# State products that leave one operand in a bank, two projection steps ahead of them, and GpSimd's low parts behind the written state

## The reference

```python
def _s5_direction(u_ctx, u_lat, lam, dt, bmat, cmat):
    lam_dt = lam * dt[:, None]
    lam_bar = jnp.exp(lam_dt)
    b_bar = ((lam_bar - 1.0) / lam)[..., None] * bmat
...
    def step(h, u_chunk):
        bu = jnp.einsum('btgs,gps->btgp', u_chunk.astype(jnp.complex64), b_bar)
        a = jnp.broadcast_to(lam_bar, bu.shape)
        _, xs = lax.associative_scan(_ssm_combine, (a, bu), axis=1)
        xs = xs + powers[None] * h[:, None]
        y = jnp.einsum('btgp,gsp->btgs', xs, cmat).real
        return xs[:, -1], y
```

## Time and profile before

| | |
|---|---|
| median of 3 runs | 2220.47 us (2219.76 to 2221.86) |
| the profiled execution | 2218.46 us, span 2216.7 us |
| TensorE busy | 2086.7 us (94%) |
| VectorE busy | 1271.0 us (57%) |
| ScalarE busy | 766.5 us (35%) |
| POOL busy | 632.0 us (29%) |
| granted TensorE clock | 0.981 of full |
| the S5 states | first product at 1358.5 us, last written at 1662.6 us |

### The profile page before, as it was taken

How to read it: one execution, slowest core, us unless ns; L and a number is a source line. 1 busy time by engine, 2 the same in 40 slices (tenths; PEclk the granted TensorE clock), 3 DMA queues, 4 the chain that set the end, 5 groups by cost and what they waited for, 6 DMA issues and landing times.

```text
span 2216.7 us, 38909 instructions
## 1 busy us (share of the span) xinstructions
PE 2086.7 (94%) x15596; PEld 1510.8 (68%) x15596; DVE 1271.0 (57%) x1896; ACT 766.5 (35%) x1425; POOL 632.0 (29%) x1129
## 2 busy tenths in 40 slices
PE   7999898999998999999989978999979999999997
PEld 6887777755554555555556547888867788888785
DVE  3366664459994444444467766999992333333334
ACT  3335543231103444444410036544444332222223
POOL 2643111500016888888701211111121000000000
PEclk9999999999999999999999989999999999999999
DMA  9221443423452111111135425999964233323321
GB/s 359 83 88 60 145 154 124 161 79 121 164 180 86 53 53 53 53 55 70 53 143 212 164 79 151 299 301 297 291 206 150 86 96 97 102 96 95 96 86 38
DMA packets 119411, 292.42 MB, mean 132 GB/s; under 512 B 11616, under 2 KB 57056, under 8 KB 113088
## 3 DMA queue, kind: packets, MB, share of 16 engines
q1 hardware_dynamic: 107072, 226.10, 31.4%
q0 software_dynamic: 12160, 63.84, 7.8%
HBM read 223.97 MB, written 65.93 MB: 131 GB/s over the span
## 4 chain that ended last, share of the span: by engine, by line
PE 82%; DVE 10%; issue 3%; ACT 3%; POOL 1%; DMA 0%; SPq 0%; DVEq 0%; ACTq 0%; POOLq 0%
PE psum L470 29%; PE psum L1867 8%; PE psum L2563 7%; PE psum L2306 5%; PE psum L2342 5%; PE psum L2737 4%; PE psum L2317 3%; PE psum L1142 3%; PE psum L2331 2%; PE psum L2387 2%; PE psum L2378 2%; DVE early L2937 2%; PE psum L304 2%; DVE early L2917 2%; DVE const L2950 1%
## 5 line engine op out<-in xcount | busy, mean ns | idle before, releaser
L470 PE MATMUL psum<-split,w_split 128*128 128x512 f32 x1632 | 371.5, 389 | 0.0
L470 PEld LDWEIGHTS psum<-split,w_split 128*128 128x128 f32 x1632 | 306.3, 188 | 63.7
L452 DVE TENSOR_TENSOR w_split<-ring,w_split 128x512 fp32r<-128x512 f32 x182 | 129.0, 709 | 309.3 <-ACT w_split L447 308.9
L2088 POOL TENSOR_TENSOR early<-early 128x8 f32<-128x8 f32 (+6 forms) x672 | 277.6, 413 | 52.8
L447 ACT ACTIVATE w_split<-ring 128x512 fp32r<-128x512 f32 x182 | 115.1, 633 | 337.0 <-PE psum L470 334.0
L1867 PE MATMUL psum<-early,ring 128*128 128x512 f32 (+1 forms) x544 | 176.5, 486 | 0.0
L2563 PE MATMUL psum<-gate,ring 128*128 128x512 f32 (+1 forms) x512 | 165.4, 486 | 1.2 <-issue 1.2
L2737 PE MATMUL psum<-h,u_w 128*128 128x256 f32 (+1 forms) x768 | 151.7, 349 | 15.1 <-ACT u_t L2651 11.4
L1867 PEld LDWEIGHTS psum<-early,ring 128*128 128x128 f32 x544 | 103.7, 191 | 71.8 <-issue 64.7
L2563 PEld LDWEIGHTS psum<-gate,ring 128*128 128x128 f32 x512 | 97.2, 190 | 69.3 <-issue 62.7
L470 PE MATMUL psum<-h,w_split 128*128 128x512 f32 x552 | 134.5, 404 | 8.0 <-DVE w_split L452 8.0
(11 more groups left out here) (439 smaller groups left out, 3511.9 us busy)
## 6 DMA issues: line engine op xcount, KB each, us to landing
ring<-in_s_glu SPq DMA_DIRECT2D x64, 512.0 KB, 3.5
ring<-in_w_mod SPq DMA_DIRECT2D x48, 512.0 KB, 5.8
made_c_pow<-area POOLq DMA_DIRECT2D x16, 1152.0 KB, 5.0
c_pow<-made_c_pow SPq DMA_DIRECT2D x32, 576.0 KB, 5.3
ring<-in_s_in SPq DMA_DIRECT2D x32, 512.0 KB, 6.4
made_b_pow<-area POOLq DMA_DIRECT2D x15, 1024.0 KB, 4.5
b_pow<-made_b_pow SPq DMA_DIRECT2D x15, 1024.0 KB, 10.2
ring<-in_w_in SPq DMA_DIRECT2D x25, 512.0 KB, 3.6
```

The source lines that it names most:

```text
L452: nc.vector.tensor_tensor(rounded(buffer(u, 1)), source(u), buffer(u, 0), ALU.subtract).then_inc(dve_done, 1)
L470: ins = nc.tensor.matmul(out, rounded(buffer(u, w)[:, ks]), values(x, k), start=(first and k == 0 and n == 0), stop=(last and k == UNIT_K ...
L2088: nc.gpsimd.tensor_tensor(o, a, b, op).then_inc(pool_done, 1)
```

## The change

Seven things change, all in the S5 stage.

1. The sine product comes first, and the cosine product is written back over its input in the banks. The add and the subtract read the one operand from the banks and the other from `mod_s`. `x_read` is counted at the subtract, not at the second product.
2. The decay has two buffers, ScalarE makes it first in its turn for a quad, and waits for the scan two quads back.
3. `x_pe(q + 1)` stands behind two projection steps; each half of a tile has four steps.
4. POOL waits for the written state of quad u - 8 before it makes the low part of unit u.
5. `y_out` has one half as its only buffer; its room goes to the second decay. The GELU of tile m waits for the store of tile m - 1.
6. The other small tiles in the same room move.
7. A second memset clears the first column of the second decay.

```diff
@@ -2612,17 +2612,17 @@
         s5 = ExitStack()
         eye = const[:, len(MASKS) * P + N_LAGS + 8 * C_LAT:len(MASKS) * P + N_LAGS + 8 * C_LAT + GS]
         lag_m = early_part(0, 2048).rearrange("p (b g c) -> p b g c", b=2, c=P)
-        y_out = early_part(2048, 1024).rearrange("p (b t) -> p b t", b=2)
-        y_tm = early_part(3072, 1024).rearrange("p (s c) -> p s c", s=STEP)
-        b_pow_t = early_part(4096, 1024).rearrange("p (b j c) -> p b j c", b=2, c=P)
-        s5_tmp = early_part(5120, 16 * C_ALL)
+        y_out = early_part(2048, 512)
+        y_tm = early_part(2688, 1024).rearrange("p (s c) -> p s c", s=STEP)
+        b_pow_t = early_part(3712, 1024).rearrange("p (b j c) -> p b j c", b=2, c=P)
+        s5_tmp = early_part(4736, 16 * C_ALL)
         b_bar_split = early_part(B_SPLIT, 4 * TPD * GS).rearrange("p (r t e i) -> p r t e i", r=2, t=TPD, e=2)
         c_pow = sb(s5, "c_pow", [2, 2, TPD, STEP + 1, GS])
         b_pow = sb(s5, "b_pow", [2, 2, TPD, STEP, GS])
         table = sb(s5, "table", [2, 2, TPD, C_ALL])
         u_w = sb(s5, "u_w", [4, 2, HALF_SLOT])
         u_t = sb(s5, "u_t", [2, TPD, C_CTX + C_ALL])
-        decay = sb(s5, "decay", [4, C_ALL])
+        decay = [sb(s5, "decay", [4, C_ALL]), early_part(6272, 4 * C_ALL).rearrange("p (g c) -> p g c", g=4)]
         u_cm = [sb(s5, "u_cm", [STEP, C_CTX + C_ALL]), early_part(6656, 1024).rearrange("p (s c) -> p s c", s=STEP)]
@@ -2681,7 +2681,9 @@
                     rest(k - 1)
             rest(KD - 1)
 
-            v.memset(decay[:, :, 0:1], 0.0).then_inc(dve_done, 1)
+            v.memset(decay[0][:, :, 0:1], 0.0).then_inc(dve_done, 1)
+            dve_count.up()
+            v.memset(decay[1][:, :, 0:1], 0.0).then_inc(dve_done, 1)
             dve.wait_ge(dve_done, dve_count.up("s5", "decay_zero"))
 
         def eye_dve(dve):
@@ -2873,10 +2875,10 @@
         def decay_act(act, q):
             if q >= QUADS:
                 return
-            if q >= 1:
-                act.wait_ge(*at("s5", "scanned", q - 1))
+            if q >= 2:
+                act.wait_ge(*at("s5", "scanned", q - 2))
             for g in range(4):
-                nc.scalar.activation(decay[:, g, 1:C_ALL], mask("ones")[:, 1:C_ALL], ACT.Copy,
+                nc.scalar.activation(decay[q % 2][:, g, 1:C_ALL], mask("ones")[:, 1:C_ALL], ACT.Copy,
                                      scale=decay8[:, 4 * q + g:4 * q + g + 1]).then_inc(act_done, 1)
                 act_count.up("s5", "decay", q)
 
@@ -2922,19 +2924,19 @@
                                           .broadcast_to([P, 2, 4, b - a]))
             dve.wait_ge(*ready(table_ready[h], m))
             dve.wait_ge(*at("s5", "x", q))
-            v.tensor_tensor(mod_c, x, both_parts(0, 0, C_ALL), ALU.mult).then_inc(dve_done, 1)
+            v.tensor_tensor(mod_s, x, both_parts(1, 0, C_ALL), ALU.mult).then_inc(dve_done, 1)
             dve_count.up()
-            tt(mod_s, x, both_parts(1, 0, C_ALL), ALU.mult, "s5", "x_read", q)
-            v.tensor_tensor(mod_c[:, 0, :, :], mod_c[:, 0, :, :], mod_s[:, 1, :, :], ALU.add).then_inc(dve_done, 1)
+            tt(x, x, both_parts(0, 0, C_ALL), ALU.mult)
+            v.tensor_tensor(mod_c[:, 0, :, :], x[:, 0, :, :], mod_s[:, 1, :, :], ALU.add).then_inc(dve_done, 1)
             dve_count.up()
-            tt(mod_c[:, 1, :, :], mod_c[:, 1, :, :], mod_s[:, 0, :, :], ALU.subtract)
+            tt(mod_c[:, 1, :, :], x[:, 1, :, :], mod_s[:, 0, :, :], ALU.subtract, "s5", "x_read", q)
             if between is not None:
                 between()
             dve.wait_ge(*at("s5", "decay", q))
             zs = mod_s
             for ri in range(2):
                 line = lambda ap: ap[:, ri, :, :].rearrange("p g c -> p (g c)")
-                v.tensor_tensor_scan(line(zs), decay[:, :, :].rearrange("p g c -> p (g c)"), line(mod_c), 0.0,
+                v.tensor_tensor_scan(line(zs), decay[q % 2][:, :, :].rearrange("p g c -> p (g c)"), line(mod_c), 0.0,
                                      ALU.mult, ALU.add).then_inc(dve_done, 1)
                 dve_count.up("s5", "scanned", q)
             dve.wait_ge(*at("s5", "scanned", q))
@@ -2996,15 +2998,16 @@
 
         def y_turn_act(act, m):
             act.wait_ge(*at("s5", "y_turned", m))
-            if m >= 2:
-                act.wait_ge(y_stored[m % 2], 16 * (m // 2))
-            nc.scalar.activation(y_out[:, m % 2, :], bank(Y_TURN_BANK),
+            if m >= 1:
+                act.wait_ge(*ready(y_stored, m - 1))
+            nc.scalar.activation(y_out, bank(Y_TURN_BANK),
                                  ACT.Gelu_apprx_tanh).then_inc(act_done, 1)
             act.wait_ge(act_done, act_count.up("s5", "yT", m))
 
 
 
-        TOKENS = (((0, 1, 2), (3, 4)), ((5,), (6, 7)))
+        STEPS_FIRST = ((0, 1), (4, 5))
+        STEPS_BEHIND = (((2,), (3,)), ((6,), (7,)))
 
         def s5_pe(pe):
             for k in range(KD):
@@ -3019,12 +3022,14 @@
                 turn_pe(pe, n)
             for q in range(QUADS):
                 m, h = divmod(q, TILE_QUADS)
+                for k in STEPS_FIRST[h]:
+                    u_project_pe(pe, m + 3, k)
                 x_pe(pe, q + 1)
                 if h == 0 and m > 0:
                     y_turn_pe(pe, m - 1)
                 for n in range(2):
                     turn_pe(pe, 2 * q + 4 + n)
-                    for k in TOKENS[h][n]:
+                    for k in STEPS_BEHIND[h][n]:
                         u_project_pe(pe, m + 3, k)
                 if h == 0:
                     lags_pe(pe, m + 1)
@@ -3054,6 +3059,7 @@
             turn_act(act, 3)
             for q in range(QUADS):
                 m, h = divmod(q, TILE_QUADS)
+                decay_act(act, q + 1)
                 if h == 0 and m > 0:
                     y_turn_act(act, m - 1)
                 turn_act(act, 2 * q + 4)
@@ -3065,7 +3071,6 @@
                     u_act(act, m + 3)
                 else:
                     lags_act(act, m + 1)
-                decay_act(act, q + 1)
                 y_act(act, q)
             y_turn_act(act, KE - 1)
             for u in range(2 * (KE + GATES_AHEAD - 1), 2 * (KE + GATES_AHEAD)):
@@ -3074,6 +3079,8 @@
         def s5_pool(pool):
             last = 2 * (KE + GATES_AHEAD - 1)
             for u in range(4, last):
+                if u >= 8:
+                    pool.wait_ge(*at("s5", "x_in", u - 8))
                 u_w_pool(pool, u)
                 if u % 2 == 1 and u >= 11:
                     y_store_pool(pool, u // 2 - 5)
@@ -3082,12 +3089,12 @@
                 u_w_pool(pool, u)
             for i in range(2):
                 pool.wait_ge(y_stored[i], 16 * KE // 2)
-            nc.gpsimd.memset(y_out[:, 0, 0:1], 0.0).then_inc(pool_done, 1)
+            nc.gpsimd.memset(y_out[:, 0:1], 0.0).then_inc(pool_done, 1)
             pool.wait_ge(pool_done, pool_count.up("s5", "y_stored"))
 
         def y_store_pool(pool, m):
             pool.wait_ge(*at("s5", "yT", m))
-            pool.dma_start(io["y"][m], y_out[:, m % 2, :]).then_inc(y_stored[m % 2], 16)
+            pool.dma_start(io["y"][m], y_out).then_inc(y_stored[m % 2], 16)
 
         FIRST_LAST = KE - 7
 
```

## The result

The changed kernel takes 2202.14 us (median of 4 runs, 2199.6 to 2205.66) against 2220.85 for the kernel before: ratio 0.9917, 95% interval 0.99 to 0.9934. The forecast was 2202. The number is right, but part of that is luck: in the stage that changes, the forecast put a gain of 18.4 us, and the profiles show 15.3. Two wrong terms cancel in part, two more are off, and the medians differ by some 3 us more than the stage does, which no part of the change explains. Which parts of the change earn the gain also came out otherwise than the text above suggests.

The account below looks back on a forecast made before the run. VectorE was taken to set S5's pace at 18.9 us a tile, TensorE close behind. Gains of 5.9 (tiles 0 to 8), 5.9 (9 to 12) and 6.6 us (13 to 15), together 18.4, took 2220.5 to 2202; range 2194 to 2213.

Parts of the forecast that it names:

- VectorE is stalled 1.0 us a quad by POOL: S5 state products: POOL's low part blocks one all-SBUF product, losing 1.0 us a quad, 2.0 us a tile.
- TensorE becomes the bound: S5 tiles: VectorE's need falls from 18.9 to 15.8 us, so TensorE's 18.05 us a tile binds.
- TensorE's work is the same: Projection steps moved to four a half: TensorE stays at 18.05 us a tile, or 17.8 if pipeline ends overlap.
- The store of y costs 0.2 us a tile: Single `y_out`: the GELU waits for the previous tile's store, making tiles 18.25 us.
- The room of 5.5 us: Single `y_out`: a store of y may take 5.5 us to land unseen; earlier stores had a median of 5.7.
- Bank writes at nothing: Cosine product written into the banks: no extra VectorE time, with 0.8 us a quad kept for the range.
- ScalarE's decay and the lags: VectorE's waits of 0.60 us for the decay and 0.54 us for the lags both go, leaving 15.8 us a tile.
- Who sets POOL's start: Where TensorE leads, ScalarE's rounding sets POOL's start, 1.5 to 3 us into the next state; up to 1.3 us blocked.
- The tail: Tiles 13 to 15, led by VectorE: six stalls of 1.0 us and some 0.6 us idle go, gaining 6.6 us.
- Tile 0: Counted among tiles 0 to 8, each going from 18.9 to 18.25 us, together 5.9 us.
- Transfers as the bound: Rival: DMA can't feed S5 tiles in under 18.9 us, giving 2210.5 us; chance 10%.
- The clock: Behind S5 TensorE runs at its lower level, granted 0.54; no gain counted, up to 3 us at the low end.

Follow-up runs that it names:

- f: The kernel before with only TensorE's new order: four projection steps a half, two ahead of `x_pe`; 2205.0 us, ratio 0.9931.
- e: The changed kernel with its products back in SBUF and `x_read` counted at the second product; 2203.1 us, ratio 0.993.
- h: The changed kernel with the old order of projection steps and the products back in SBUF; 2203.2 us, ratio 0.993.
- n: The changed kernel with three projection steps ahead of `x_pe` and one behind the first transposition; 2206.8 us, ratio 0.9947.
- c: The kernel before with one edit only, POOL's wait for the written state before each low part; 2199.0 us, ratio 0.9909.
- g: The kernel before with POOL's wait for the state and the four projection steps of a half in one run; 2203.7 us, ratio 0.9932.
- m: The changed kernel with the four projection steps of a half in one run behind `x_pe` and products back in SBUF; 2199.4 us, ratio 0.9916.
- d: The changed kernel without POOL's wait for the written state; 2201.6 us, ratio 0.9924.

## Why the prediction was right, and where it was not

*VectorE is stalled 1.0 us a quad by POOL: right.* In every kernel that moves the low part behind the written state, by the wait or by the order, the state products fall to 0.43 us at most (f keeps two long ones). Where the low part then meets an add, a scan or L2142 with its operands in SBUF, that one is held. The Trainium skill says the same ("SBUF — State Buffer", "Who interferes with whom"): two SBUF inputs contend with a GpSimd instruction that reads SBUF, one doesn't. The traces agree: e and the changed kernel are the pair that shows it, 1.18 against 0.56 us for the add.

*TensorE becomes the bound: right.* It is busy 18.40 of 18.40 us.

*"TensorE's work is the same", 18.05 us a tile: this step failed.* The same matmuls took 18.43 us. In the old order, with no wait left, they take 17.77 (h), the 17.8 that the prediction had in brackets: so the 18.05 of before held some 0.3 us of pipeline ends, as the profile models them, at its two waits. The new order costs 0.66 us a tile: two more runs of steps 0.35, y ahead of steps 0.20, L2907 behind steps 0.10. Shown by h, f (the order alone gives 18.42) and n.

*The store of y costs 0.2 us a tile: wrong, 0.* The room of 5.5 us was right (5.5 from the store at 1487.34 to the Gelu at 1492.87), but the stores landed in 4.4. These two errors cancel in part in tiles 1 to 8, 18.25 forecast against 18.43; in tiles 1 to 12 they leave 2.5 us of gain that did not come.

*Bank writes at nothing: right* (956 ns). The 65 ns more for a PSUM source, estimated from the Trainium skill ("VectorE: DVE Perf Modes", "The TRN2 errata"), isn't seen: the subtract takes 548 ns with one bank operand and took 0.55 us with none.

*ScalarE's decay and the lags: half right.* The wait for the decay went. The wait for the lags did not, against the sign that the prediction named: it grew from 0.54 to 2.42 us a tile, because VectorE is ahead of TensorE, which makes them. Neither matters in the middle tiles, where c keeps both waits and has a shorter tile than the changed kernel. With one run a half the decay does matter (g against m).

*Who sets POOL's start: told as a caveat, and it is the rule.* In the middle tiles the wait for the state never holds POOL, and without it nothing is lost there or in the tail (d). The stall went because the two steps ahead of x push the rounding behind the state. POOL's wait (c) and the order (f) are two ways to the same thing, each enough for nearly all of it; together they give no more, and the order costs 0.48 us a tile against c.

*The tail: mis-sized,* 3.7 us for 6.6. Two of the six stalls stayed, at L2142 and in the last scan, where the wait for the state does not keep POOL off; and the 0.6 us of idle time was not there, for VectorE's timeline of before has no gap from 1610.38 on. *Tile 0* gave 3.0 where 0.65 was put, for TensorE's bound was applied to it.

*Transfers as the bound: refuted.* c moves 321 GB/s in a tile where before moved 302. *The clock:* still low behind the stage (granted 0.52 from 1648 to 1655), no gain, as said.

What stays open: why the medians differ by 18.7 us where the stage and the profiled executions show 15.3 and 15.7 (single executions of one kernel spread that much, so it may be chance), why the stores land faster, and what sets the start of the stage, which moves by up to 9 us among profiles. Without those 3 us the forecast of 18.4 would have been some 3 too high.

## What to carry to other kernels

When two engines are within a few per cent of each other, find the hidden stall of the one that leads (a form whose highest duration is several times its median, at the times of the other engine's instruction) and remove it by the smallest edit; here two lines did as much as the whole change. Then count the other engine's work again for the new order, start to start, because a new order of the same matmuls can cost it time (here 0.66 us of 18) even when no matmul is added. A single buffer behind a store is safe only as long as the queue ahead of the store and its landing fit before the next write to the buffer: here 1.3 us more cost the whole gain.

## What was not expected of the hardware

What a block of matmuls costs on TensorE depends on its neighbours: a transposition followed by y or lags takes 0.17 us more from start to start than one followed by a projection step (0.53 against 0.35 us), y followed by a step 0.10 more than y followed by L2907's matmuls, and eight steps take 0.35 us more in six runs than in four. A store of the same 256 KB landed in 4.4 us in the median where it took 5.7 before, issued only a little elsewhere in the tile. And a POOL instruction of 1.29 us that starts 0.03 us before a scan holds it for 1.1 us.
